# Tail of a decoder step: last expert result copied by two engines, samples combined first and scaled by GpSimd, prompt tiles scaled and stored in halves

## The chip, the cores and the metric

The kernel runs on one core of a Trainium2 chip. The core has TensorE (matrix products, results in PSUM banks ps0 to ps7), VectorE, ScalarE, GpSimd and SyncE, each with its own instruction stream, which meet only at semaphores. SyncE does nothing here but issue transfers. The metric is the device time of one launch in microseconds; lower is better. In the profile PE is TensorE, DVE VectorE, ACT ScalarE, POOL GpSimd and SP SyncE.

## The reference

One decoder layer for 256 prompt tokens and 8 sample tokens (one new token of each of 8 sequences), model width 1024, all in float32: a mixer, a cross-attention, 32 routed experts of which each token takes 4, and a last RMS norm. The end of it is what matters here:

```python
def run_block(args):
    e, idx = args
    xb = x_pad[idx]
    gu = xb @ w_e1[e] + b_e1[e]
    ...
    h = (u + 1.0) * (g * jax.nn.sigmoid(SWIGLU_ALPHA * g))
    return h @ w_e2[e] + b_e2[e]
...
x = x + routed_experts(rms_norm(x, g_moe), moe_w)      # each token: sum over its 4 experts, weighted by gates
...
y_prompt = rms_norm(xp, g_final)                       # x * rsqrt(mean(x*x) + EPS) * g_final
y_sample = rms_norm(xs, g_final)
```

## The kernel before

The work is written out engine by engine. The 32 experts are done in 16 pairs (`PAIRS`), each expert on up to 64 token slots (`CAP`): 8 slots for the samples, 56 for prompt tokens that were gathered by a selection matrix. SyncE streams each expert's weights (first matrix in four transfers, second in two, 2 MB each) through the tile `ring` and two more places. For each expert TensorE multiplies by the first matrix (`up`, L1737), VectorE and ScalarE apply the gated activation, TensorE turns the result (`turn_h`, L1746) and multiplies by the second matrix (`down`, L1756) into bank ps3: 64 slots in partitions 0 to 63 for columns 0 to 511, and in partitions 64 to 127 for columns 512 to 1023. ScalarE's `keep_y` (L779) copies the two halves to `ysb`; the pair's second expert takes rows 64 to 127 of `ysb`.

The running result is the tile `tok`: prompt tiles 0 and 1 (128 tokens each, `tok[:, 0, :]` and `tok[:, 1, :]`) and the samples (`tok[0:8, 2, :]`). A pair's `ysb` is brought back to the prompt tokens by a product with the gates `gT`, two halves of 512 columns for each tile, and VectorE adds them to `tok`. For the last pair these are the lines after `pair(PAIRS - 1)`: TensorE L1820 (four products, one semaphore step of `comb_done` each), VectorE L1268 (four adds). The samples' share of the last pair is two products with `pick_last` (TensorE L1823, added onto what `early_samples` has already put in ps4 and ps5) and two adds (VectorE L1273).

Then comes the last norm, tile by tile. ScalarE squares with a sum (L825) and takes the root (L828); it does the tiles in the order 0, 1, samples. VectorE takes the reciprocal (L1303) and multiplies the whole tile by it and by the final gain `gfin`, which lies in SBUF (L1305). SyncE stores each tile behind it (L444, L446) and waits for all. Each engine works in order. GpSimd loads the bias of each expert (L508) and has nothing more to do after that. Where a routing overflows the slots, a loop over more blocks follows (`n > 0`); in the profiled execution it is passed over.

Of the kernel before, what the change touches and what calls it, by code (L numbers as in the profile page):

```python
# [117 lines left out]
def build(nc, a, outs):  # L118
    ctx = ExitStack()
    with ctx:  # L120
# [168 lines left out]
        smp_chain gates8_ready acc_zeroed sel_ready selg_ready gathered xe_ready gt_turned gt_ready g_clamped u_clamped t_done tu_done h_ready  # L289
        h_turned hT_ready y_ready comb_done acc_done b1_filled b1_used gfin_loaded  # L290
        fin_sq fin_sd fin_rec fin_ready y_stored""".split()
# [31 lines left out]
        def _(sp):  # L323
# [118 lines left out]
            for t in range(2):  # L442
                sp.wait_ge(S["fin_ready"], t + 1)
                sp.dma_start(outs["y_prompt"][0, t * P:(t + 1) * P, :], tok[:, t, :]).then_inc(S["y_stored"], 16)  # L444
            sp.wait_ge(S["fin_ready"], 3)
            sp.dma_start(outs["y_sample"].rearrange("b t d -> (b t) d"), tok[0:NB, 2, :]).then_inc(S["y_stored"], 16)  # L446
            sp.wait_ge(S["y_stored"], 48)
# [6 lines left out]
        def _(pool):  # L454
# [65 lines left out]
            with pool.If(n > 0):  # L520
                pool.wait_ge(S["table_ready"], 1)
                with pool.Fori(0, n) as j:
                    e = pool.value_load(tabi[0:1, 0, bass.ds(j, 1)], min_val=0, max_val=NE - 1)
                    pool.wait_ge(S["b1_used"], j + NE)
                    bias(e)


        @block.scalar
        def _(act):
# [245 lines left out]
            def keep_y(b, e2):  # L775

                act.wait_ge(S["freed"], RING * b + (freed_after(MOE0 - 1) + RING))
                for i in range(2):
# [12 lines left out]
            def pair(q, last=False):  # L791
# [9 lines left out]
                keep_y(2 * q + 1, 1)  # L801
# [18 lines left out]
            for t, (t0, rows) in enumerate(TT):  # L820
# [6 lines left out]
                act.wait_ge(S["fin_sq"], t + 1)  # L827
# [4 lines left out]
        def _(dve):  # L832
# [430 lines left out]
            pair(PAIRS - 1, True)  # L1263
            for t in range(2):
# [5 lines left out]
            dve.wait_ge(S["smp_chain"], 3 + PAIRS)  # L1270
            for i in range(2):
                dst = tok[0:NB, 2, 512 * i:512 * i + 512]
                last = dve.tensor_tensor(dst, dst, ps[LAST_BANKS[2] + i][0:NB, :], ALU.add)  # L1273
            last.then_inc(S["smp_chain"], 1)
# [25 lines left out]
            for t, (t0, rows) in enumerate(TT):  # L1300
                r = slice(0, rows)
                dve.wait_ge(S["fin_sd"], t + 1)
                dve.reciprocal(frs[:, t:t + 1], frs[:, t:t + 1]).then_inc(S["fin_rec"], 1)  # L1303
                dve.wait_ge(S["fin_rec"], t + 2)
                dve.scalar_tensor_tensor(out=tok[r, t, :], in0=tok[r, t, :], scalar=frs[r, t:t + 1], in1=gfin[r, :],  # L1305
                                         op0=ALU.mult, op1=ALU.mult).then_inc(S["fin_ready"], 1)
# [3 lines left out]
        def _(pe):  # L1310
# [506 lines left out]
            pe.wait_ge(S["y_ready"], NE)  # L1817
# [57 lines left out]
```

## Time and profile before

| | us |
|---|---|
| median of 3 runs | 1221.78 (1220.18 to 1224.59) |
| the profiled execution, its own time | 1222.58 |
| its span, first to last instruction | 1221.0 |
| TensorE busy | 1144.9 (94%) |
| VectorE busy | 337.5 (28%) |
| ScalarE busy | 186.2 (15%) |
| GpSimd busy | 45.5 (4%) |
| transfers | 457.43 MB, mean 375 GB/s |

The span counts the instructions of the core; the execution's own time has 1.58 us more around it. Busy shares are means over the whole span; what the end of the kernel waits for is read from the chain of waits and the timeline, whose times count from the start of the span.

### The profile page before, as it was taken

The numbers are of one execution on the slowest core, as the hardware profiler recorded it, in microseconds if no ns is written. First come the engines' busy times: TensorE is split into PE (matmuls) and PEld (weight loads), VectorE is DVE, ScalarE is ACT, GpSimd is POOL, SyncE is SP. The second block draws the span as 40 slices with busy tenths as digits, with TensorE's granted clock in tenths as the row PEclk, the third lists the DMA queues.
The fourth block names the chain that finished last, engine by engine and source line by source line (L and its number), as shares of the span: only waits on it lengthen the run. The fifth ranks groups of instructions, "written<-read, shape, count | busy, mean of one in ns | idle before, by whom it ended". The sixth has DMA issues, their size and how long they took to land.

```text
span 1221.0 us, 14241 instructions
## 1 busy us (share of the span) xinstructions
PE 1144.9 (94%) x5466; PEld 550.5 (45%) x5466; DVE 337.5 (28%) x828; ACT 186.2 (15%) x364; POOL 45.5 (4%) x85
## 2 busy tenths in 40 slices
PE   9999999999999999999989898989898999989896
PEld 7887888684334343333323232323232333333322
DVE  4795529134120212122120202021212121212113
ACT  4205213322011110101101010101010101010102
POOL 4100002000000000000000000000000000000000
PEclk9999999998899999999999999999999999999999
DMA  9398335995999999999999999999999999999993
GB/s 299 109 321 264 142 104 193 390 414 215 420 426 425 429 425 429 428 429 426 428 429 427 427 428 429 427 426 429 428 428 428 427 428 429 429 427 428 426 428 146
DMA packets 65624, 457.43 MB, mean 375 GB/s; under 512 B 5515, under 2 KB 34435, under 8 KB 40885
## 3 DMA queue, kind: packets, MB, share of 16 engines
q1 hardware_dynamic: 62576, 452.00, 90.0%
q10 hardware_dynamic: 1165, 3.04, 0.7%
q0 software_dynamic: 1856, 2.02, 0.6%
q8 instruction: 18, 0.29, 0.1%
q14 instruction: 9, 0.07, 0.0%
HBM read 453.71 MB, written 3.81 MB: 375 GB/s over the span
## 4 chain that ended last, share of the span: by engine, by line
DMA 48%; PE 44%; DVE 5%; ACT 2%; issue 1%; POOL 0%; SPq 0%; ACTq 0%; DVEq 0%; POOLq 0%
DMA ring<-in_w_e 48%; PE ps L1737 17%; PE ps L1400 10%; PE ps L1756 5%; PE ps L1422 3%; DVE ring L1072 2%; PE ps L1713 1%; PE ps L1704 1%; PE ps L1642 1%; PE ps L1340 1%; PE ps L1585 1%; PE ps L1554 1%; PE ps L1314 1%; PE ps L1633 1%; PE ps L1746 1%
## 5 line engine op out<-in xcount | busy, mean ns | idle before, releaser
L1737 PE MATMUL ps<-ring,mixed 128*64 128x512 f32 x1536 | 347.1, 597 | 38.6 <-DMA ring<-in_w_e 38.5
L1756 PE MATMUL ps<-ring,mixed 128*64 128x512 f32 x1024 | 229.7, 602 | 0.7 <-issue 0.7
L1737 PEld LDWEIGHTS ps<-ring,mixed 128*64 128x64 f32 x1536 | 104.6, 137 | 265.3 <-issue 181.0
L1227 DVE TENSOR_SCALAR mixed<-ps 128x512 f32<-128x512 f32 x32 | 22.1, 692 | 590.5 <-PE ps L1737 590.5
L1756 PEld LDWEIGHTS ps<-ring,mixed 128*64 128x64 f32 x1024 | 71.8, 138 | 156.6 <-issue 144.4
L769 ACT ACTIVATE mixed<-mixed 128x512 f32<-128x512 f32 x32 | 20.2, 630 | 516.1 <-DVE mixed L1227 516.1
L1713 PEld LDWEIGHTS ps<-mixed 128*128 128x128 f32 x512 | 63.4, 199 | 24.5 <-issue 24.3
L779 ACT ACTIVATE mixed<-ps 64x512 f32<-64x512 f32 x64 | 37.8, 591 | 229.2 <-PE ps L1756 228.8
L1713 PE MATMUL ps<-mixed 128*128 128x128 f32 x512 | 69.2, 290 | 0.0
L1737 PE MATMUL ps<-mixed 128*64 128x512 f32 x256 | 58.2, 596 | 9.4 <-DMA mixed<-in_w_e 9.4
L1214 DVE SCALAR_TENSOR_TENSOR mixed<-mixed,gates 128x1024 f32<-128x1024 f32 x15 | 19.3, 1285 | 153.2 <-ACT mixed L779 153.2
L1400 PE MATMUL ps<-mixed,ring 128*128 128x264 f32 x256 | 57.6, 387 | 0.4 <-DVE mixed L1106 0.4
L1737 PE MATMUL ps<-low,mixed 128*64 128x512 f32 x256 | 57.9, 593 | 0.0
L1422 PE MATMUL ps<-ring,low 128*128 128x256 f32 x256 | 56.2, 380 | 0.0
L1704 PE MATMUL ps<-mixed 128*128 128x512 f32 x120 | 55.5, 606 | 0.0
L1400 PEld LDWEIGHTS ps<-mixed,ring 128*128 128x128 f32 x256 | 48.6, 190 | 9.1 <-issue 0.6
L1422 PEld LDWEIGHTS ps<-ring,low 128*128 128x128 f32 x256 | 48.7, 190 | 6.5
L508 POOL DMA_DIRECT2D mixed<-in_b_e x32 | 18.2, 567 | 866.9 <-PE ps L1642 849.8
L945 DVE SCALAR_TENSOR_TENSOR mixed<-mixed,par 128x256 f32<-128x256 f32 x120 | 47.6, 468 | 0.0
L1400 PE MATMUL ps<-sq,ring 128*128 128x264 f32 x192 | 44.8, 398 | 0.0
L1400 PEld LDWEIGHTS ps<-sq,ring 128*128 128x128 f32 x192 | 37.6, 196 | 6.7
L1208 DVE TENSOR_TENSOR tok<-tok,ps 128x512 f32<-128x512 f32 x64 | 39.6, 680 | 0.2 <-PE ps L1702 0.2
(320 smaller groups left out, 769.0 us busy)
## 6 DMA issues: line engine op xcount, KB each, us to landing
ring<-in_w_e SPq DMA_DIRECT2D x160, 2048.0 KB, 23.4
low<-in_w_e SPq DMA_DIRECT2D x15, 2048.0 KB, 27.6
mixed<-in_w_e SPq DMA_DIRECT2D x15, 2048.0 KB, 31.9
ring<-in_w_in SPq DMA_DIRECT2D x8, 1024.0 KB, 16.3
ring<-in_cache_mem_k SPq DMA_DIRECT2D x8, 1024.0 KB, 4.8
ring<-in_cache_mem_v SPq DMA_DIRECT2D x7, 1024.0 KB, 7.6
ring<-in_w_k SPq DMA_DIRECT2D x4, 1024.0 KB, 8.7
ring<-in_w_v SPq DMA_DIRECT2D x4, 1024.0 KB, 12.4
```

What stands on the lines that cost most here:

```text
L769: act.activation(tg, g1, ACT.Tanh, scale=ALPHA / 2).then_inc(S["t_done"], 1)
L779: m = act.activation(ysb[CAP * e2:CAP * e2 + CAP, 512 * i:512 * i + 512], ps[3][CAP * i:CAP * i + CAP, :], ACT.Copy)
L945: dve.scalar_tensor_tensor(out=gc[:, c, 0:SEQ], in0=gpad[:, c, bass.ds(w, SEQ)], scalar=par[:, bass.ds(4 * w + (C_WCF + c), 1)], in1=gc[:, ...
L1072: last = dve.tensor_tensor_reduce(key[:, t, h, :], key[:, t, h, :], qb[h][:, HD * b:HD * b + HD], 1.0, 0.0, ALU.mult, ALU.add, sT[:, t, 4 ...
L1208: last = dve.tensor_tensor(dst, dst, ps[bank + i][0:rows, :], ALU.add)
L1227: dve.tensor_scalar(g1, ps[0][:, :], LIMIT, None, ALU.min).then_inc(S["g_clamped"], 1)
L1400: m = pe.matmul(ps[o % 4][:, 0:TOK], wslot(n)[:, k, half * P:(half + 1) * P], (xn if o < 4 else sq)[:, k, :] if kind == "in" else src(k), ...
L1422: m = pe.matmul(ps[KV_BANK[j]][:, 256 * t:256 * t + 256], mn[:, k, P * t:P * t + P], wslot(n)[:, k, :], start=(k == 0), stop=(k == KD - 1))
L1704: m = pe.matmul(ps[bank + i][:, :], gT[:, t0:t0 + P], ysb[:, cols], start=True, stop=True)
L1713: m = pe.matmul(ps[4 + i][:, P * (k % 4):P * (k % 4) + P], xnt[:, t, DEAL[k]], sel[:, t, :], start=(t == 0), stop=(t == 1))
L1737: m = pe.matmul(ps[gu][CAP * i:CAP * i + CAP, :], xeT[:, k, CAP * e2:CAP * e2 + CAP], w[:, D * gu + 512 * i:D * gu + 512 * i + 512], start ...
L1756: m = pe.matmul(ps[3][CAP * i:CAP * i + CAP, :], hTv[:, k % 4, CAP * (k // 4):CAP * (k // 4) + CAP], ring[:, s, D * (k % 2) + 512 * i:D * ...
```

## The change

It has four parts. The last expert's result is copied by ScalarE (columns 0 to 511) and by VectorE (columns 512 to 1023). The samples' products and adds of the last pair are put ahead of those of the prompt tiles, and ScalarE squares the samples first. The samples' last scaling is taken from VectorE and given to GpSimd, as two operations. VectorE scales each prompt tile in two halves of 512 columns, and SyncE stores each half by itself, with the sample store between the two tiles.

```diff
--- before.py
+++ after.py
@@ -286,9 +286,9 @@
         late_loaded qs_turned qs_kept dots_done rs_ready qrow_loaded qb_ready s_chain spv_done osb_kept pick_chain
         o_done part_kept tok_rooted tm_turned tokr_kept xnt_kept logit_done lg_zeroed lg_ready idx_ready eq_ready gate_chain rank_chain block_chain nblk_ready v0_ready ge_ready mask_ready rank_done
         gt0_turned gt0_kept be2_loaded tab_turned tab_ready table_ready
-        smp_chain gates8_ready acc_zeroed sel_ready selg_ready gathered xe_ready gt_turned gt_ready g_clamped u_clamped t_done tu_done h_ready
+        smp_chain gates8_ready acc_zeroed sel_ready selg_ready half_kept gathered xe_ready gt_turned gt_ready g_clamped u_clamped t_done tu_done h_ready
         h_turned hT_ready y_ready comb_done acc_done b1_filled b1_used gfin_loaded
-        fin_sq fin_sd fin_rec fin_ready y_stored""".split()
+        fin_sq fin_sd fin_rec smp_fin fin_ready y_stored""".split()
         S = {n: sem(n) for n in names}
 
         def slot(n):
@@ -439,12 +439,14 @@
                         fill(e, s, used(j + NE - 1, s + 1))
                     rest(e, j + NE)
 
-            for t in range(2):
-                sp.wait_ge(S["fin_ready"], t + 1)
-                sp.dma_start(outs["y_prompt"][0, t * P:(t + 1) * P, :], tok[:, t, :]).then_inc(S["y_stored"], 16)
-            sp.wait_ge(S["fin_ready"], 3)
-            sp.dma_start(outs["y_sample"].rearrange("b t d -> (b t) d"), tok[0:NB, 2, :]).then_inc(S["y_stored"], 16)
-            sp.wait_ge(S["y_stored"], 48)
+            for i in range(4):
+                if i == 2:
+                    sp.wait_ge(S["smp_fin"], 2)
+                    sp.dma_start(outs["y_sample"].rearrange("b t d -> (b t) d"), tok[0:NB, 2, :]).then_inc(S["y_stored"], 16)
+                t, cols = i // 2, slice(512 * (i % 2), 512 * (i % 2) + 512)
+                sp.wait_ge(S["fin_ready"], i + 1)
+                sp.dma_start(outs["y_prompt"][0, t * P:(t + 1) * P, cols], tok[:, t, cols]).then_inc(S["y_stored"], 16)
+            sp.wait_ge(S["y_stored"], 80)
             sp.wait_ge(S["kv_stored"], 32)
             sp.wait_ge(S["rows_stored"], 16 * 6)
             sp.wait_ge(S["caches_shifted"], 32)
@@ -523,6 +525,13 @@
                     e = pool.value_load(tabi[0:1, 0, bass.ds(j, 1)], min_val=0, max_val=NE - 1)
                     pool.wait_ge(S["b1_used"], j + NE)
                     bias(e)
+
+
+            pool.wait_ge(S["gfin_loaded"], 16)
+            pool.wait_ge(S["fin_rec"], 2)
+            pool.tensor_scalar(tok[0:NB, 2, :], tok[0:NB, 2, :], frs[0:NB, 2:3], None, ALU.mult).then_inc(S["smp_fin"], 1)
+            pool.wait_ge(S["smp_fin"], 1)
+            pool.tensor_tensor(tok[0:NB, 2, :], tok[0:NB, 2, :], gfin[0:NB, :], ALU.mult).then_inc(S["smp_fin"], 1)
 
 
         @block.scalar
@@ -772,10 +781,10 @@
                 act.wait_ge(S["h_turned"], b + 1)
                 act.activation(hT, ps[2][:, :], ACT.Copy, scale=0.5).then_inc(S["hT_ready"], 1)
 
-            def keep_y(b, e2):
+            def keep_y(b, e2, shared=False):
 
                 act.wait_ge(S["freed"], RING * b + (freed_after(MOE0 - 1) + RING))
-                for i in range(2):
+                for i in range(1 if shared else 2):
                     m = act.activation(ysb[CAP * e2:CAP * e2 + CAP, 512 * i:512 * i + 512],
                                        ps[3][CAP * i:CAP * i + CAP, :], ACT.Copy)
                 m.then_inc(S["y_ready"], 1)
@@ -798,7 +807,7 @@
                 keep_h(2 * q + 1)
                 if not last:
                     keep_gathered(q + 1)
-                keep_y(2 * q + 1, 1)
+                keep_y(2 * q + 1, 1, last)
 
             with act.Fori(0, PAIRS - 1) as q:
                 pair(q)
@@ -817,14 +826,15 @@
 
             act.wait_ge(S["fin_rec"], 1)
             act.activation(unused, eps[:, 0:1], ACT.Sqrt)
-            for t, (t0, rows) in enumerate(TT):
+            for step, t in enumerate((2, 0, 1)):
+                rows = TT[t][1]
                 if t < 2:
                     act.wait_ge(S["acc_done"], 2 * n + (2 * PAIRS + 1 + t))
                 else:
                     act.wait_ge(S["smp_chain"], 3 + PAIRS + 1)
                 act.activation(xnt[0:rows, t, :], tok[0:rows, t, :], ACT.Square,
                                accum_out=fss[0:rows, t:t + 1]).then_inc(S["fin_sq"], 1)
-                act.wait_ge(S["fin_sq"], t + 1)
+                act.wait_ge(S["fin_sq"], step + 1)
                 act.activation(frs[:, t:t + 1], fss[:, t:t + 1], ACT.Sqrt, bias=eps[:, 0:1], scale=1.0 / D).then_inc(S["fin_sd"], 1)
 
 
@@ -1261,17 +1271,19 @@
             with dve.Fori(1, PAIRS - 1) as q:
                 pair(q)
             pair(PAIRS - 1, True)
+            dve.wait_ge(S["freed"], RING * (NE - 1) + (freed_after(MOE0 - 1) + RING))
+            dve.tensor_copy(ysb[CAP:2 * CAP, 512:D], ps[3][CAP:2 * CAP, :]).then_inc(S["half_kept"], 1)
+            dve.wait_ge(S["smp_chain"], 3 + PAIRS)
+            for i in range(2):
+                dst = tok[0:NB, 2, 512 * i:512 * i + 512]
+                last = dve.tensor_tensor(dst, dst, ps[LAST_BANKS[2] + i][0:NB, :], ALU.add)
+            last.then_inc(S["smp_chain"], 1)
             for t in range(2):
                 for i in range(2):
                     dve.wait_ge(S["comb_done"], 2 * PAIRS + 2 * t + i + 1)
                     dst = tok[:, t, 512 * i:512 * i + 512]
                     last = dve.tensor_tensor(dst, dst, ps[LAST_BANKS[t] + i][:, :], ALU.add)
                 last.then_inc(S["acc_done"], 1)
-            dve.wait_ge(S["smp_chain"], 3 + PAIRS)
-            for i in range(2):
-                dst = tok[0:NB, 2, 512 * i:512 * i + 512]
-                last = dve.tensor_tensor(dst, dst, ps[LAST_BANKS[2] + i][0:NB, :], ALU.add)
-            last.then_inc(S["smp_chain"], 1)
             n = dve.value_load(nblk[0:1, 0:1], min_val=0, max_val=P)
             with dve.If(n > 0):
                 dve.wait_ge(S["tab_ready"], 2)
@@ -1297,13 +1309,16 @@
                         add_round(2 * j + (2 * PAIRS + 4), t, PAIR_BANKS[t])
 
             dve.wait_ge(S["gfin_loaded"], 16)
-            for t, (t0, rows) in enumerate(TT):
-                r = slice(0, rows)
-                dve.wait_ge(S["fin_sd"], t + 1)
+            for step, t in enumerate((2, 0, 1)):
+                dve.wait_ge(S["fin_sd"], step + 1)
                 dve.reciprocal(frs[:, t:t + 1], frs[:, t:t + 1]).then_inc(S["fin_rec"], 1)
-                dve.wait_ge(S["fin_rec"], t + 2)
-                dve.scalar_tensor_tensor(out=tok[r, t, :], in0=tok[r, t, :], scalar=frs[r, t:t + 1], in1=gfin[r, :],
-                                         op0=ALU.mult, op1=ALU.mult).then_inc(S["fin_ready"], 1)
+                if t == 2:
+                    continue
+                dve.wait_ge(S["fin_rec"], step + 2)
+                for i in range(2):
+                    cols = slice(512 * i, 512 * i + 512)
+                    dve.scalar_tensor_tensor(out=tok[:, t, cols], in0=tok[:, t, cols], scalar=frs[:, t:t + 1], in1=gfin[:, cols],
+                                             op0=ALU.mult, op1=ALU.mult).then_inc(S["fin_ready"], 1)
 
 
         @block.tensor
@@ -1815,13 +1830,14 @@
                 pair(q)
             pair(PAIRS - 1, last=True)
             pe.wait_ge(S["y_ready"], NE)
+            pe.wait_ge(S["half_kept"], 1)
+            for i in range(2):
+                m = pe.matmul(ps[LAST_BANKS[2] + i][0:NB, :], pick_last, ysb[:, 512 * i:512 * i + 512], start=False, stop=True)
+            m.then_inc(S["smp_chain"], 1)
             for t in range(2):
                 for i in range(2):
                     pe.matmul(ps[LAST_BANKS[t] + i][:, :], gT[:, P * t:P * t + P], ysb[:, 512 * i:512 * i + 512],
                               start=True, stop=True).then_inc(S["comb_done"], 1)
-            for i in range(2):
-                m = pe.matmul(ps[LAST_BANKS[2] + i][0:NB, :], pick_last, ysb[:, 512 * i:512 * i + 512], start=False, stop=True)
-            m.then_inc(S["smp_chain"], 1)
             pe.wait_ge(S["nblk_ready"], 1)
             n = pe.value_load(nblk[0:1, 0:1], min_val=0, max_val=P)
             with pe.If(n > 0):
```

What follows is the order of instructions before and after on the engines concerned; the brackets name semaphores. First TensorE, from the last down projection to the end of the products, before:

```order
L1756 MATMUL ps<-ring,mixed 64x512 [waits filled8,hT_ready,gt_ready]
L1756 MATMUL ps<-ring,mixed 64x512 x7
L1756 MATMUL ps<-ring,mixed 64x512 [waits filled10]
L1756 MATMUL ps<-ring,mixed 64x512 x7
L1820 MATMUL ps<-mixed 128x512 [waits y_ready]
L1820 MATMUL ps<-mixed 128x512 x3
L1823 MATMUL ps<-mixed,extra 8x512 x2
```

and after the change:

```order
L1771 MATMUL ps<-ring,mixed 64x512 [waits filled8,hT_ready,gt_ready]
L1771 MATMUL ps<-ring,mixed 64x512 x7
L1771 MATMUL ps<-ring,mixed 64x512 [waits filled10]
L1771 MATMUL ps<-ring,mixed 64x512 x7
L1835 MATMUL ps<-mixed,extra 8x512 [waits half_kept,y_ready]
L1835 MATMUL ps<-mixed,extra 8x512
L1839 MATMUL ps<-mixed 128x512 x4
```

The two sample products (8x512) have moved ahead of the four prompt products (128x512), and they now wait for `half_kept`, VectorE's copy, as well as for `y_ready`, ScalarE's.

VectorE from its last activation to the end of the adds, before:

```order
L1230 SCALAR_TENSOR_TENSOR mixed<-mixed 128x512 [waits t_done]
L1233 SCALAR_TENSOR_TENSOR mixed<-mixed 128x512 [waits u_clamped,tu_done]
L1268 TENSOR_TENSOR tok<-tok,ps 128x512 [waits comb_done] x4
L1273 TENSOR_TENSOR tok<-tok,ps 8x512 [waits smp_chain]
L1273 TENSOR_TENSOR tok<-tok,ps 8x512
```

and after:

```order
L1240 SCALAR_TENSOR_TENSOR mixed<-mixed 128x512 [waits t_done]
L1243 SCALAR_TENSOR_TENSOR mixed<-mixed 128x512 [waits u_clamped,tu_done]
L1275 COPY mixed<-ps 64x512 [waits freed]
L1279 TENSOR_TENSOR tok<-tok,ps 8x512 [waits smp_chain]
L1279 TENSOR_TENSOR tok<-tok,ps 8x512
L1285 TENSOR_TENSOR tok<-tok,ps 128x512 [waits comb_done] x4
```

The copy of 64x512 is new, and the sample adds stand ahead of the four prompt adds.

VectorE in the last norm, before:

```order
L1303 RECIPROCAL small<-small 128x1 [waits fin_sd,gfin_loaded]
L1305 SCALAR_TENSOR_TENSOR tok<-tok,small,xn 128x1024 [waits fin_rec]
L1303 RECIPROCAL small<-small 128x1 [waits fin_sd]
L1305 SCALAR_TENSOR_TENSOR tok<-tok,small,xn 128x1024 [waits fin_rec]
L1303 RECIPROCAL small<-small 128x1 [waits fin_sd]
L1305 SCALAR_TENSOR_TENSOR tok<-tok,small,xn 8x1024 [waits fin_rec]
```

and after:

```order
L1314 RECIPROCAL small<-small 128x1 [waits fin_sd,gfin_loaded]
L1314 RECIPROCAL small<-small 128x1 [waits fin_sd]
L1320 SCALAR_TENSOR_TENSOR tok<-tok,small,xn 128x512 [waits fin_rec]
L1320 SCALAR_TENSOR_TENSOR tok<-tok,small,xn 128x512
L1314 RECIPROCAL small<-small 128x1 [waits fin_sd]
L1320 SCALAR_TENSOR_TENSOR tok<-tok,small,xn 128x512 [waits fin_rec]
L1320 SCALAR_TENSOR_TENSOR tok<-tok,small,xn 128x512
```

The two reciprocals that come first are those of the samples and of tile 0; the scaling of 8x1024 is gone, and each of the two wide ones is two of 512 columns. Both operations of the samples are now GpSimd's last (a scaling that waits for `fin_rec`, a product that waits for the scaling by `smp_fin`).

## Rows read from the trace of the kernel before

**Rows 1.** The page, its chain that ended last, shares of the span by engine.

```profile
DMA 48%; PE 44%; DVE 5%; ACT 2%; issue 1%; POOL 0%; SPq 0%; ACTq 0%; DVEq 0%; POOLq 0%
```

**Rows 2.** The chain in order of time, end of the kernel: start us, us, what.

```profile
1165.67 25.61 DMA ring<-in_w_e
...
1199.37 7.10 PE ps L1756 x32
```

**Rows 3.** Timeline of the tail: start us, us, engine line operation, [idle before <-releaser].

```profile
1206.49 1.19 ACT L779 ACTIVATE mixed<-ps 64x512 f32<-64x512 f32 x2 [7.22 <-PE ps L1756]
...
1207.74 3.70 PE L1820 MATMUL ps<-mixed 128*128 128x512 f32 x8 [1.28 <-ACT mixed L779]
...
1208.90 0.69 DVE L1268 TENSOR_TENSOR tok<-tok,ps 128x512 f32<-128x512 f32 x1 [11.07 <-PE ps L1820]
...
1210.48 1.06 ACT L825 ACTIVATE mixed<-tok 128x1024 f32<-128x1024 f32 x1 [1.28 <-DVE tok L1268]
...
1211.37 1.88 PE L1823 MATMUL ps<-mixed,extra 128*8 128x512 f32 x4
...
1211.48 0.69 DVE L1268 TENSOR_TENSOR tok<-tok,ps 128x512 f32<-128x512 f32 x1 [0.17 <-PE ps L1820]
1211.66 0.29 ACT L828 ACTIVATE small<-small,eps 128x1 f32<-128x1 f32 x1
...
1213.29 1.27 DVE L1273 TENSOR_TENSOR tok<-tok,ps 8x512 f32<-8x512 f32 x2 [1.12 <-PE ps L1823]
...
1214.52 0.16 DVE L1303 RECIPROCAL small<-small 128x1 f32<-128x1 f32 x1
...
1214.71 1.29 DVE L1305 SCALAR_TENSOR_TENSOR tok<-tok,small,xn 128x1024 f32<-128x1024 f32 x1
...
1217.50 1.27 DVE L1305 SCALAR_TENSOR_TENSOR tok<-tok,small,xn 8x1024 f32<-8x1024 f32 x1
1218.80 0.34 SPq L446 DMA_DIRECT2D out_y_sample<-tok  x1
```

**Rows 4.** Waits of SyncE from 1150 us: us in total, times, longest us.

```profile
SPq L120 <- DMA out_y_sample<-tok: 1.3, 1, 1.3
```

**Rows 5.** A window of the tail: us; engines busy; PEclk, DMA share, GB/s.

```profile
1217.00:1217.50 0.50, 0.00 (x0) 0.00 (x0) 0.47 (x2) 0.00 (x0) 0.00 (x0) 0.50 0.97 401
```

**Rows 6.** VectorE's groups by shape: count, busy us, mean ns, idle before.

```profile
L1102 DVE COPY mixed<-ps 128x512 f32<-128x512 f32 x2 | 1.3, 686 | 9.8 <-PE ps L1585 9.8
L1022 DVE COPY sq<-ps 11x512 f32<-11x512 f32 x1 | 0.7, 671 | 0.0
L1230 DVE SCALAR_TENSOR_TENSOR mixed<-mixed 128x512 f32<-128x512 f32 x32 | 22.1, 692 | 3.2
```

**Rows 7.** GpSimd's groups by line, at 1024 columns.

```profile
L501 POOL PARTITION_BROADCAST mixed<-mixed x4 | 5.3, 1391 | 152.3 <-DMA mixed<-tok 152.3
L514 POOL MEMSET mixed<- 128x1024 f32 x1 | 0.9, 946 | 41.5 <-ACT mixed L731 41.5
```

**Rows 8.** Timeline in the attention part, VectorE beside GpSimd.

```profile
188.69 2.83 POOL L501 PARTITION_BROADCAST mixed<-mixed  x2 [4.62 <-DMA mixed<-tok]
...
188.98 1.37 DVE L1072 CUSTOM_DVE_ANT_0 ring<-ring,mixed 128x256 f32<-128x256 f32 x1
...
190.28 1.37 DVE L1072 CUSTOM_DVE_ANT_0 ring<-ring,mixed 128x256 f32<-128x256 f32 x1
...
191.58 0.41 DVE L1072 CUSTOM_DVE_ANT_0 ring<-ring,mixed 128x256 f32<-128x256 f32 x1
```

**Rows 9.** Lines L501 and L1072: duration ns min/median/max, first and last start.

```profile
L501 POOL PARTITION_BROADCAST mixed<-mixed x4: 1297/1370/1527, 181.6 to 190.1; - x4
...
L1072 DVE CUSTOM_DVE_ANT_0 ring<-ring,sq x16: 412/414/1371, 198.7 to 206.3; 128x256 f32<-128x256 f32 x16
```

**Rows 10.** Timeline of GpSimd, start-up and its last instruction before the tail.

```profile
27.29 0.18 POOL L474 IOTA iota_s<- 128x56 f32 x1 [7.17 <-issue]
...
1141.41 0.56 POOL L508 DMA_DIRECT2D mixed<-in_b_e  x1 [28.48 <-PE ps L1642]
```

## Prediction

> **What bounds the kernel now.** I read the page first: the chain that ended last runs through transfers for 48% of the span, nearly all of it expert weights, and through TensorE for 44% [rows 1]. The chain of waits in order of time shows where that ends: the last transfer that anything waits for is over at 1191.28 (1165.67 + 25.61), and from then on it is one serial stretch of some 30 us, in which the last down projection ends at 1206.47 [rows 2]. The change touches nothing ahead of that point, so the 1206.5 us before it stay, and the whole question is what the last 14.5 us become.
>
> The timeline of that tail [rows 3] is to be read as four steps. (a) ScalarE copies both halves of the last result in 1.19 us; TensorE starts at 1207.74. (b) Four prompt products, one each 0.86 us (VectorE's four adds start from 1208.90 to 1211.48), then two sample products from 1211.37; VectorE's sample add starts at 1213.29, 1.92 after its products began. (c) VectorE has its first scaled square root at 1211.95 (1211.66 + 0.29) but is held in order by the sample add until 1214.52. (d) Three scalings of about 1.28 us follow back to back, the small sample one last, and end at 1218.77. SyncE issues the sample store at 1218.80, takes 0.34, waits 1.3 for its landing [rows 4], so it is released at 1220.44; another 0.56 closes the span of 1221.0. The two prompt stores move at about 401 GB/s [rows 5] and are hidden until nearly the end.
>
> **Step (a), two engines copy.** ScalarE keeps one 64x512 copy (half of 1.19, so 0.60); VectorE takes the other. The trace has no 64-row copy by VectorE, but a 128x512 one from PSUM takes 0.686 and an 11x512 one 0.671 [rows 6], so rows don't matter and I take 0.67. Both start at 1206.49, TensorE starts at 1206.49 + 0.67 + 0.05 = 1207.21 in place of 1207.74: 0.53 earlier. Bounds: if the two engines hinder each other in the one bank, 0.6 later than that and the gain is nothing.
>
> **Step (b), samples first.** A first add started 1.16 after TensorE (1208.90 - 1207.74) and each further one 0.86 later, so two products are ready 2.02 after the start: sample add at 1209.23, its two parts take 1.27, end 1210.50. Prompt products are ready at 1210.09, 1210.95, 1211.81 and 1212.67; the adds of 0.69 then start at 1210.53, 1211.24, 1211.95 and 1212.69, the last ends at 1213.38. That is 1.21 later than before (1211.48 + 0.69 = 1212.17). ScalarE needs 1.47 a tile (1210.48 to 1211.95): samples from 1210.54 to 1212.01, tile 0 to 1213.50, tile 1 to 1214.99. Nothing on VectorE is held by the sample add any more, yet its first wide scaling now waits for tile 0's root at 1213.50, against 1214.71 at which it started before.
>
> **Step (d) without any interference.** VectorE: sample reciprocal at about 1213.35 for 0.16; tile 0's from 1213.53, scaling at 1213.72. A half takes 0.69 (a 128x512 of this form: 0.692 [rows 6]), so fin halves at 1214.41 and 1215.10; tile 1's reciprocal to 1215.28, its halves at 1216.00 and 1216.69. That is 2.08 ahead of 1218.77, half of it from the sample scaling of 1.27 that left VectorE, the rest from the 1.0 earlier start, less two more fixed costs.
>
> **GpSimd's two operations.** The scaling of 8x1024 and the product with the final gain are new to this engine, and no row has either. Rows are no shorter for few partitions on the other engines (8x1024 takes 1.27 like 128x1024). Nearest rows at 1024 columns [rows 7]: a memset, which reads nothing, 0.95; a broadcast, which reads one input, 1.39. For the one-input scaling I take 1.2, between the two. For the two-input product the floor is 0.95, the ceiling twice the broadcast, 2.75; I take 2.1, since it must read twice. The Trainium skill, GPSIMD Engine Reference, section "Elementwise — side-by-side cycle accounting", states some 2.6 cycles an element for a two-input operation; at the clock on that page this is an estimate of 2.2 us, no run here shows it, and the sum below would end 0.1 later by it.
>
> **Do they hold VectorE up?** Here is the term that decides the sign. In the attention part, VectorE runs a chain of 128x256 operations with two SBUF inputs, each 0.41. While GpSimd runs two broadcasts from 188.69 for 2.83, exactly two of them take 1.37 instead, and the next is back at 0.41 [rows 8]. Nor is that one place: of the sixteen such operations on the next head, beside later broadcasts, the longest took 1.371 at a median of 0.414 [rows 9]. So such an operation isn't slowed in proportion: it waits for nearly the whole GpSimd operation, one per GpSimd operation, and ends 0.13 behind it (the first broadcast took the 1.53 that [rows 9] give as the longest, so 190.22, against 190.35). The wide scaling also reads two SBUF inputs, tile and gain. By these rows its price is: GpSimd's scaling runs 1213.60 to 1214.80; the first half, begun at 1213.72, ends some 0.4 behind it (0.69 less the 0.28 that the blocked 0.41 had already done) at 1215.2. GpSimd's product, ready at 1214.9, gets its turn then, 1215.2 to 1217.3, as the second broadcast did; the second half ends at 1217.7. Reciprocal and two halves free of it: 1217.9, 1218.6, 1219.3. So the 2.08 gained turn into 0.55 lost on VectorE. If the second half gets ahead of the product instead, the product holds tile 1's first half, and the end is the same.
>
> The Trainium skill, SBUF — State Buffer, section "Who interferes with whom", says that a VectorE instruction with two SBUF inputs and a GpSimd instruction that reads SBUF exclude each other for the whole instruction, whoever is first. By that rule, with no overlap at all, both blocked halves would end 0.28 later, so the sum would be 0.56 higher than by the row; the row is what I go by. The adds from PSUM have one SBUF input and are free of it.
>
> **The stores.** In the new order SyncE issues tile 0's halves, then waits for the sample result (1217.3, long before tile 1), then tile 1's halves. So the last issue is at 1219.33. From issue to release the sample store took 1.64; a half tile has 0.23 MB more, 0.57 at 401 GB/s, so 1.64 to 2.2, and I take 1.9. Sum: 1219.33 + 1.9 + 0.56 = 1221.8, against 1221.0: **0.8 us slower** in the profiled execution (own time 1222.58, so 1223.4). That execution stands 0.80 above the median of the runs, 1221.78; on that footing the forecast is 1222.6. Ends: both GpSimd operations at 0.95 and the store at 1.64 give a last half at 1217.9 and a span of 1220.1 (0.9 faster); 1.39 with 2.75 and 2.2 give 1220.1 and 1222.9 (1.9 slower).
>
> **Rivals.**
> 1. No hold-up: the form of scaling here doesn't exclude GpSimd (for it: the rows are of another VectorE operation and another GpSimd operation, and GpSimd works on 8 partitions only). Then VectorE is done at 1216.69, but SyncE waits in order for the sample result at 1213.60 + 1.2 + 0.1 + 2.1 = 1217.0 and issues tile 1's halves at 1217.35 and 1217.7; 1217.7 + 1.9 + 0.56 = 1220.2, 0.8 faster: 1221.0. With GpSimd at 0.95 each it isn't late at all and 1.8 is gained: 1220.0.
> 2. Slower beyond what can be told: GpSimd's first arithmetic after a long pause stalls. The one unexplained GpSimd idle time is 7.17 ahead of an iota, put down to issue [rows 10]. The same here puts the sample result at 1213.6 + 7.2 + 3.3 = 1224.1, and tile 1's stores are queued behind it on SyncE: last issue 1224.8, span 1227.3, 6.3 slower: 1228.1. It crosses 0.3% (3.7 us, about what a measurement of this kernel can tell from no change) only where the stall is over 4.6. Against it: that idle time stood in the start-up, behind a string of transfers issued by the same engine, and here its last issue is at 1141, over 70 us before.
> 3. The shared copy brings nothing (one bank read by two engines): everything 0.5 to 0.6 later than the forecast, 1223.2. Against it: they read different partitions.
>
> **How the numbers follow.** Hold-up as forecast 0.70, no hold-up 0.22, GpSimd stall 0.03, copy brings nothing 0.05. All but the stall lie within 0.3%: the tail has 14.5 us, and no mechanism in it pays or costs 3.7 except that one. So faster 0.03 and slower 0.03 for what the spread between runs (1220.18 to 1224.59) may feign. Range: from rival 1's 1220.0 to the forecast's upper bound, 1222.6 + 1.1 = 1223.7, each widened by some of that spread: 1219.7 to 1224.4. The forecast's own range is 1220.9 to 1223.7.
>
> **What the changed profile would show.** Right: TensorE's sample products at 1207.2 if the down projection ends at 1206.5; four scalings of which two take well over 1 us and two 0.69; GpSimd's two at 1.2 and 2.1; SyncE's last store issue at about 1219.3. Wrong: all four scalings at 0.69 (rival 1), and then the gap before the sample store on SyncE tells whether GpSimd is the new bound; a GpSimd start long after the sample reciprocal (rival 2). The result would be off too if the part before 1206.5 moved by more than the tail can, which would be spread, not this change.

## The result, and the profile after

The changed kernel takes 1226.76 us (median of 20 runs, 1225.60 to 1229.02) against 1222.22 us before (20 runs, 1220.18 to 1225.41): the ratio is 1.0038, 95% interval 1.0032 to 1.0044. That is 4.5 us slower, where 0.8 slower was forecast, and outside the range of 1219.7 to 1224.4.

Since the part before the tail moves by some microseconds from run to run, the tail is compared by itself in all that follows: the time from the end of the last down projection to the end of the span. The chain of waits gives its start (start us, us, what). After the change:

```profile
1164.47 25.62 DMA ring<-in_w_e
...
1198.17 7.10 PE ps L1771 x32
...
1212.91 0.23 DVE small L1314 x2
1213.15 0.14 issue
1213.29 3.37 POOL tok L532
1216.65 0.04 issue
1216.69 2.47 POOLq L120
```

The projection ends at 1205.27, the span at 1223.9: a tail of **18.6 us**, against 14.5 before (1221.0 less 1206.47, [rows 2]). So the tail is 4.1 longer, which is the result but for 0.4, well within the spread of runs. The chain now ends in GpSimd, and its last piece isn't named for an operation but for L120, the end of the program. The timeline of the tail after the change (start us, us, engine line operation, idle before):

```profile
1205.30 0.69 DVE L1275 COPY mixed<-ps 64x512 f32<-64x512 f32 x1 [8.66 <-PE ps L1771]
1206.14 1.88 PE L1835 MATMUL ps<-mixed,extra 128*8 128x512 f32 x4 [0.88 <-DVE mixed L1275]
...
1211.68 0.69 DVE L1285 TENSOR_TENSOR tok<-tok,ps 128x512 f32<-128x512 f32 x1 [0.17 <-PE ps L1839]
...
1212.91 0.22 DVE L1314 RECIPROCAL small<-small 128x1 f32<-128x1 f32 x2 [0.54 <-issue]
1213.17 2.27 DVE L1320 SCALAR_TENSOR_TENSOR tok<-tok,small,xn 128x512 f32<-128x512 f32 x2
1213.29 3.37 POOL L532 TENSOR_SCALAR tok<-tok,small 8x1024 f32<-8x1024 f32 x1 [72.48 <-DVE small L1314]
...
1215.55 1.41 DVE L1320 SCALAR_TENSOR_TENSOR tok<-tok,small,xn 128x512 f32<-128x512 f32 x2
1216.73 2.43 POOL L534 TENSOR_TENSOR tok<-tok,xn 8x1024 f32<-8x1024 f32 x1
1219.19 0.34 SPq L445 DMA_DIRECT2D out_y_sample<-tok  x1
1219.57 0.83 SPq L448 DMA_DIRECT2D out_y_prompt<-tok  x2
```

Beside [rows 3]: TensorE starts 0.87 behind the projection, not 1.27, so the shared copy gains 0.4. VectorE is done at 1216.96, which is 11.7 behind the projection and 0.6 sooner than before. One of its four halves took 1.60, the others some 0.75 (ns min/median/max):

```profile
L1320 DVE SCALAR_TENSOR_TENSOR tok<-tok,small,xn x4: 743/751/1604, 1213.2 to 1216.2; 128x512 f32<-128x512 f32 x4
```

But GpSimd's scaling takes 3.37 us, and its product ends at 1219.16; SyncE has tile 1's two halves ready since 1216.3 and 1216.96 and issues them behind the sample store from 1219.57. And then the line L120, which holds the end of each engine's program (duration ns min/median/max, start):

```profile
L120 DVEq DRAIN  x1: 1449/1449/1449, 1215.6 to 1215.6; - x1
L120 POOLq DRAIN  x1: 6967/6967/6967, 1216.7 to 1216.7; - x1
L120 SPq COMPARE_BRANCH  x1: 41/41/41, 1222.6 to 1222.6; - x1
L120 SPq DRAIN  x1: 13/13/13, 1222.7 to 1222.7; - x1
...
L120 POOLq EVENT_SEMAPHORE  x2: 17/17/17, 1223.7 to 1223.8; - x2
```

SyncE sees its last store landed at 1222.6. GpSimd's drain starts with its product and runs 6.97 us, to 1223.66, 4.5 behind the product's end; only then do the engines meet and the span closes. The trace of before has a drain too, at a place where it cost nothing. It stood behind a transfer issue there, and ended 7.2 behind it (1141.41 + 0.56, [rows 10]):

```profile
L120 POOLq DRAIN  x1: 6642/6642/6642, 1142.5 to 1142.5; - x1
L120 SPq COMPARE_BRANCH  x1: 41/41/41, 1220.6 to 1220.6; - x1
```

So three things stand in the tail after: operations of GpSimd that are longer than forecast, stores that queue behind them on SyncE, and the drain. The first two make one path, which ends in SyncE's release; the drain makes another. In the trace of before the span ends 0.4 behind the release (1220.6, 1221.0). Counted so, SyncE's path would end the changed kernel at 1223.0, a tail of 17.7; the drain ends it at 1223.9, a tail of 18.6. So the trace puts 3.2 us of the loss on the late stores and only the last 0.9 on the drain, if the drain counts at all. The experiments test that.

### The profile page after: what moved, and what is told of

It reads as the page before. It is cut to its first block, busy times and chain, and to the rows that moved or that the text cites. A ratio compares the mean times of both kernels' runs of the same rounds, so it can differ in the third digit from the quotient of the medians.

```text
span 1223.9 us, 14250 instructions
## 1 busy us (share of the span) xinstructions
PE 1142.3 (93%) x5466; PEld 548.7 (45%) x5466; DVE 338.0 (28%) x830; ACT 185.2 (15%) x363; POOL 51.5 (4%) x87
## 4 chain that ended last, share of the span: by engine, by line
DMA 48%; PE 44%; DVE 5%; ACT 1%; issue 1%; POOL 0%; POOLq 0%; SPq 0%; ACTq 0%; DVEq 0%
DMA ring<-in_w_e 48%; PE ps L1752 17%; PE ps L1415 10%; PE ps L1771 5%; PE ps L1437 3%; DVE ring L1082 2%; PE ps L1728 1%; PE ps L1719 1%; PE ps L1657 1%; PE ps L1355 1%; PE ps L1600 1%; PE ps L1329 1%; PE ps L1569 1%; PE ps L1761 0%; PE ps L1648 0%
## 5 line engine op out<-in xcount | busy, mean ns | idle before, releaser
L1752 PEld LDWEIGHTS ps<-mixed 128*64 128x64 f32 x256 | 17.5, 137 | 49.2 <-issue 30.8
```

The lines of the kernel that those rows point to most:

```text
L1752: m = pe.matmul(ps[gu][CAP * i:CAP * i + CAP, :], xeT[:, k, CAP * e2:CAP * e2 + CAP], w[:, D * gu + 512 * i:D * gu + 512 * i + 512], start ...
```

## The experiments

Each kernel is the changed one or the one before with one edit. Tails are from one profiled execution of each. Kernels whose tails end with the same work came out within 0.1 of each other: 14.5 in two, 18.5 to 18.6 in three.

**The sample store last.** Edit on SyncE:

```diff
-                if i == 2:
-                    sp.wait_ge(S["smp_fin"], 2)
-                    sp.dma_start(outs["y_sample"]..., tok[0:NB, 2, :])
...
+            sp.wait_ge(S["smp_fin"], 2)
+            sp.dma_start(outs["y_sample"]..., tok[0:NB, 2, :])
```

> The changed kernel with one thing moved: SyncE stores the samples last instead of between the two prompt tiles. Tail is the time from the end of the last down projection to the end of the span: 14.5 us before the change, 18.6 after. Drain theory (GpSimd's own drain at the end of its program ends some 4.5 us behind its last operation and closes the span): tile 1's two stores are issued about 3 us earlier, SyncE is done about 1.5 us earlier, and the span does not move: tail 18.6, within 0.2. Queue theory (the stores of tile 1 held behind the sample store set the end): tail 17.0, time 1.5 us less than the changed kernel's.

1226.4 us (5 runs), ratio to the kernel before 1.0037 (1.0024 to 1.0049), the same as the change. The tail was 19.1. SyncE was released at 1220.3, and the drain ran on:

```profile
L120 POOLq DRAIN  x1: 6872/6872/6872, 1216.1 to 1216.1; - x1
L120 SPq COMPARE_BRANCH  x1: 41/41/41, 1220.3 to 1220.3; - x1
```

The queue theory falls: SyncE was done 2.7 us ahead of the drain's end (1223.0), and that gained nothing, so the drain closes the span. It doesn't follow that the queue is harmless: in the changed kernel its path ends only 0.9 ahead of the drain's. The tail is even 0.5 longer, because GpSimd's scaling took 3.95 here:

```profile
1212.02 1.42 DVE L1319 SCALAR_TENSOR_TENSOR tok<-tok,small,xn 128x512 f32<-128x512 f32 x2
1212.13 3.95 POOL L531 TENSOR_SCALAR tok<-tok,small 8x1024 f32<-8x1024 f32 x1 [72.52 <-DVE small L1313]
...
1213.54 1.99 DVE L1319 SCALAR_TENSOR_TENSOR tok<-tok,small,xn 128x512 f32<-128x512 f32 x2
```

Both engines lose here: VectorE 0.6 in its second pair of halves, GpSimd 0.6. Why it was the second pair here and the first in the changed kernel, the traces don't show.

**The samples scaled by VectorE, last.**

```diff
-            pool.tensor_scalar(tok[0:NB, 2, :], tok[0:NB, 2, :], frs[0:NB, 2:3], None, ALU.mult)
...
-            pool.tensor_tensor(tok[0:NB, 2, :], tok[0:NB, 2, :], gfin[0:NB, :], ALU.mult)
...
+                if t == 2:
+                    dve.scalar_tensor_tensor(out=tok[0:NB, 2, :], in0=tok[0:NB, 2, :], scalar=frs[0:NB, 2:3],
+                                             in1=gfin[0:NB, :], op0=ALU.mult, op1=ALU.mult)
```

> The changed kernel without GpSimd: VectorE does the samples' last scaling, in one operation, last, and SyncE stores them last; the copy by two engines, the samples' products first and the halves stay. If all of the loss is GpSimd's (drain and long operations together): tail about 14.4 us and a time within 0.1% of the kernel before. If the loss lies in the new order (samples first delays the prompt tiles) or in the halved scalings and stores: tail 15.5 or more. VectorE's halves at 0.69 us each if the 0.75 and 1.60 of the changed kernel came from GpSimd beside it; still 0.75 if a half of a row costs that.

1222.12 us (12 runs), ratio 0.9993 (0.9984 to 1.0002): no change that can be told. The tail was 14.4 (projection ended at 1207.98, span 1222.35). All of the loss is GpSimd's; the rest of the change, with the samples scaled and stored last, is worth 0.1 us together. And the halves take the same without GpSimd:

```profile
1215.82 1.41 DVE L1316 SCALAR_TENSOR_TENSOR tok<-tok,small,xn 128x512 f32<-128x512 f32 x2
...
1217.34 1.42 DVE L1316 SCALAR_TENSOR_TENSOR tok<-tok,small,xn 128x512 f32<-128x512 f32 x2
```

So 1.41 a pair is what halves cost here, and only the 2.27 of tile 0 in the changed kernel was a hold-up, of 0.86.

**A memset behind the last scaling**, in the kernel before:

```diff
+            pool.wait_ge(S["fin_ready"], 3)
+            pool.memset(extra[0:NB, 84:96], 0.0)
```

> The kernel before, with one GpSimd memset of 8x12 elements on scratch columns that waits for VectorE's last scaling; nothing waits for it but the end of the program. Drain theory: the drain behind it ends some 4.5 us after it, at about 4.7 us past the last scaling where the span of before ended 2.2 past it: 2.5 us slower, 0.2%. Rival (the long drain in the changed kernel belongs to GpSimd arithmetic or to its reads, not to a plain write): no change.

1225.49 us (11 runs), ratio 1.0022 (1.0012 to 1.0032); the tail was 17.2, 2.7 more than before. An operation of 0.1 us that nothing reads makes this kernel 0.2% slower:

```profile
1217.95 0.34 SPq L446 DMA_DIRECT2D out_y_sample<-tok  x1
1217.99 0.10 POOL L528 MEMSET extra<- 8x12 f32 x1 [76.84 <-DVE tok L1308]
```

```profile
L120 POOLq DRAIN  x1: 4602/4602/4602, 1218.0 to 1218.0; - x1
L120 SPq COMPARE_BRANCH  x1: 41/41/41, 1219.8 to 1219.8; - x1
```

Again the drain ends 4.5 behind the last operation (4.60 less 0.12), as behind the product, and SyncE had been released 2.8 before that. **The control**, the same memset some 10 us earlier:

```diff
-            pool.wait_ge(S["fin_ready"], 3)
+            pool.wait_ge(S["comb_done"], 2 * PAIRS + 1)
```

> Control for the memset behind the last scaling: the same GpSimd memset in the kernel before, but waiting for the first prompt product of the last pair, some 2.5 us behind the last down projection. Drain theory: it drains until about 7.2, far from the end, tail 14.5, time as before (within 0.1%). If an added GpSimd instruction at the end of the program costs by itself, wherever it runs: 2.5 us slower, as there.

1222.17 us (10 runs), ratio 1.0002 (0.9990 to 1.0014), tail 14.5. The memset stood at 1208.56, its drain (4602 ns again) was over at 1213.1. It is the place of GpSimd's last instruction that costs, not its presence.

**GpSimd warmed up** with a small scaling and a small product 70 us ahead, on 8x12 elements of scratch (`wu`):

```diff
+            pool.memset(wu, 1.0)
+            pool.tensor_scalar(wu, wu, ones[0:NB, 0:1], None, ALU.mult)
+            pool.tensor_tensor(wu, wu, wu, ALU.mult)
```

> The changed kernel, with a scaling and a product of 8x12 elements put on GpSimd some 70 us ahead, on scratch columns. First-use theory (2 of the 3.37 us of GpSimd's scaling are paid once): the scaling of 8x1024 takes 1.2 to 1.5, the sample result is 2 us earlier, the drain too, tail 16.6. Inherent theory (the operation costs 3.3 ns an element on this engine): it takes 3.37 again, tail 18.6.

1227.59 us (6 runs), ratio 1.0037 (1.0026 to 1.0049), tail 18.6. The first-use theory falls:

```profile
1145.75 0.10 POOL L531 MEMSET extra<- 8x12 f32 x1 [0.57 <-issue]
1153.03 0.68 POOL L533 TENSOR_SCALAR extra<-extra,ones 8x12 f32<-8x12 f32 x1 [7.18 <-issue]
1153.79 0.20 POOL L535 TENSOR_TENSOR extra<-extra 8x12 f32<-8x12 f32 x1
1217.62 3.38 POOL L538 TENSOR_SCALAR tok<-tok,small 8x1024 f32<-8x1024 f32 x1 [63.63 <-DVE small L1320]
1221.09 2.44 POOL L540 TENSOR_TENSOR tok<-tok,xn 8x1024 f32<-8x1024 f32 x1
```

From 12 to 1024 columns the scaling grows by 2.70 us, 2.7 ns a column, and the product by 2.24, 2.2 ns a column. The scaling's price is in its columns. There is a first-use cost of another kind, 7.18 us in which GpSimd stood still ahead of the small scaling. Each kernel has two configuring instructions on the scaling's line, here and in the changed kernel:

```profile
L533 POOLq MODIFY_POOL_CONFIG  x2: 1/1/1, 1145.9 to 1145.9; - x2
```

```profile
L532 POOLq MODIFY_POOL_CONFIG  x2: 5/5/5, 1141.4 to 1141.5; - x2
```

Here the 7.18 us follow them; in the changed kernel they stand at 1141.4, at the head of the 72 us in which GpSimd waited anyway, and its scaling started 0.16 behind the reciprocal. So it is most likely that the stall fell into that wait; the trace doesn't show it by itself.

**The scaling written as a product** (the first line added), **and by a constant** (the second, in another kernel).

```diff
-            pool.tensor_scalar(..., frs[0:NB, 2:3], None, ALU.mult)
+            pool.tensor_tensor(..., frs[0:NB, 2:3].to_broadcast([NB, D]), ALU.mult)
+            pool.tensor_scalar(..., 0.5, None, ALU.mult)
```

> The changed kernel with GpSimd's scaling by a number per partition written as a product with that number spread over the row (one element per partition read again and again). If the operation with a number per partition is what is slow on this engine (3.37 us): 2.4 us, like the product with the gain, tail 17.7. If the first of two late operations costs more, whichever it is: 3.3 again, tail 18.6.

> The changed kernel with GpSimd scaling the samples by the constant 0.5 in place of the reciprocal root, so y_sample is not normalised and the number per partition is not read. If a one-input operation runs near one element a cycle once no number is fetched: 1 to 1.4 us, tail 16.6. If the slowness is in the operation's loop: 3.3, tail 18.6.

Both only profiled. The kernel with the constant leaves the norm of the samples out. By the constant: 3.29, tail 18.5. As a product: tail 17.9, and the timeline:

```profile
1213.32 3.05 DVE L1320 SCALAR_TENSOR_TENSOR tok<-tok,small,xn 128x512 f32<-128x512 f32 x2
1213.38 2.43 POOL L532 TENSOR_TENSOR tok<-tok,small 8x1024 f32<-8x1024 f32 x1 [72.45 <-DVE small L1314]
...
1214.09 2.63 SPq L448 DMA_DIRECT2D out_y_prompt<-tok  x2
1215.89 2.67 POOL L534 TENSOR_TENSOR tok<-tok,xn 8x1024 f32<-8x1024 f32 x1
...
1216.47 3.30 DVE L1320 SCALAR_TENSOR_TENSOR tok<-tok,small,xn 128x512 f32<-128x512 f32 x2
```

GpSimd's operation with one input and a number is what is slow, wherever the number comes from; the product over 1024 columns needs 2.43. And here is the hold-up of the kind that was forecast: each product kept one of VectorE's halves waiting, the pairs took 3.05 and 3.30 in place of 1.41, so 1.64 and 1.89 more. The first pair ended at 1216.37, 0.56 behind the product's end at 1215.81. A half takes 0.75, so all but some 0.2 of the held half was done after GpSimd was through. It was the second half: the first was over when SyncE issued its store at 1214.09, though the product had begun at 1213.38, beside it. The scaling holds VectorE for only 0.6 to 0.9 of its 3.3 to 3.9 us.

The tail fell by 0.7 only, with the scaling 0.9 shorter: the second product took 2.67 and ended at 1218.56, and the drain again closed the span 4.7 behind it.

**The copy by two engines alone**, on the kernel before, only profiled:

> The kernel before with only the first part of the change, the last result copied by ScalarE and VectorE. The changed kernel's trace has TensorE start 0.86 us behind the last down projection where before it was 1.27, so tail 14.1 us, 0.4 less. If the copies were not on the path: 14.5.

Its edit is the diff's lines on `keep_y`, `half_kept` and the copy of 64x512. Tail 14.1 (projection ended at 1208.24, span 1222.35), TensorE started 0.87 behind the projection. This part gives its 0.4.

**Whole tiles, no GpSimd**, only profiled: the kernel in which VectorE scales the samples, with one operation and one store for each tile.

```diff
-                for i in range(2):
-                    cols = slice(512 * i, 512 * i + 512)
-                    dve.scalar_tensor_tensor(out=tok[:, t, cols], ...)
+                dve.scalar_tensor_tensor(out=tok[r, t, :], ...)
```

> The changed kernel without GpSimd and without the halves: VectorE scales tile 0, tile 1 and the samples whole, three stores, samples last. The kernel without GpSimd but with halves had a tail of 14.4 us. A half costs VectorE 0.08 us more than half a tile, twice: if the halves give nothing at the end (the sample store is last), tail 14.2 to 14.3. If the earlier first half matters for the queue of transfers: 14.6 or more.

Tail 14.1 (1208.18 to 1222.29), 0.3 less than with halves, where 0.1 to 0.2 was expected: with the sample store last the halves give nothing and cost 0.3. It is the same 14.1 as with the shared copy alone, so the samples' place ahead of the prompt tiles shows no gain either.

**GpSimd's product early, ScalarE scales.** The gain can be multiplied in before the root is known:

```diff
+            pool.wait_ge(S["smp_chain"], 3 + PAIRS + 1)
+            pool.tensor_tensor(acc[0:NB, :], tok[0:NB, 2, :], gfin[0:NB, :], ALU.mult).then_inc(S["smp_fin"], 1)
...
+            act.wait_ge(S["fin_rec"], 2)
+            act.wait_ge(S["smp_fin"], 1)
+            act.activation(acc[0:NB, :], acc[0:NB, :], ACT.Copy, scale=frs[0:NB, 2:3]).then_inc(S["smp_fin"], 1)
```

> GpSimd's work put where its drain is covered: right behind the samples' last add it multiplies the samples by the final gain into scratch (one product, 2.4 us), while ScalarE squares; ScalarE, free after the last root, scales that by the reciprocal; VectorE scales the prompt tiles in halves; SyncE stores the samples between the tiles. Drain theory: GpSimd's product starts 4.1 us behind the last down projection and ends at 6.5, its drain at 11.0, ahead of the stores; the last half is issued at 10.9, so tail 13.1 to 13.3 us, 1.3 less than before: time about 0.1% below the kernel before. If a late GpSimd product costs in another way too (it holds VectorE's adds, or its drain is longer here): tail over 14.5.

> The kernel with GpSimd's product by the gain early, ScalarE's scaling of the samples and no work of GpSimd at the end, now with the prompt tiles scaled and stored whole. With halves its tail was 13.95 us, not 13.1: SyncE was released 2.85 us behind the issue of the last half (256 KB), where the kernel before needed 2.5 from the issue of a whole tile to its last byte. If stores in halves land more slowly: last whole store issued at 10.7 us, tail 13.5, about 0.1% below the kernel before. If the landing of two stores in a row is what costs, whatever their size: 13.9 to 14.2.

With halves: 1221.53 us (11 runs), ratio 0.9995 (0.9986 to 1.0005), tail 13.9. With whole tiles: 1222.0 (11 runs), ratio 0.9992 (0.9983 to 1.0002), tail 14.3. Both misses: neither can be told from the kernel before, and the tails expected were 13.1 to 13.3, and 13.5 for whole tiles. The drain did what the theory says:

```profile
1212.07 2.36 POOL L532 TENSOR_TENSOR mixed<-tok,xn 8x1024 f32<-8x1024 f32 x1 [68.66 <-DVE tok L1280]
...
1213.40 0.69 DVE L1286 TENSOR_TENSOR tok<-tok,ps 128x512 f32<-128x512 f32 x1 [0.17 <-PE ps L1840]
...
1218.05 0.99 SPq L448 DMA_DIRECT2D out_y_prompt<-tok  x2
```

```profile
L120 POOLq DRAIN  x1: 6892/6892/6892, 1212.0 to 1212.0; - x1
L120 SPq COMPARE_BRANCH  x1: 41/41/41, 1221.4 to 1221.4; - x1
```

It was over at 1218.9, ahead of the landing, and VectorE's adds from PSUM kept their 0.69 beside the product. What took the gain is the landing: the second half was issued at 1218.71 (the pair's 0.99 ends at 1219.04, an issue is 0.33), and SyncE was released 2.7 behind that. With whole tiles the last issue was at 1214.57 and the release at 1217.9, 3.3 later; the small store that comes last in the kernel before needs 1.8. So the last issue came 1.5 and 1.7 sooner behind the projection than before, and less than half of that was paid.

What the end follows is rather the first store. It was issued at (kernel before, halves, whole tiles):

```profile
1216.03 1.73 SPq L444 DMA_DIRECT2D out_y_prompt<-tok  x2
```

```profile
1216.53 1.00 SPq L448 DMA_DIRECT2D out_y_prompt<-tok  x2
```

```profile
1213.18 0.36 SPq L447 DMA_DIRECT2D out_y_prompt<-tok  x1
```

From there to the release it is 4.6, 4.9 and 4.7 us, and in between the transfers hardly pause; with halves (us; engines busy; PEclk, DMA share, GB/s):

```profile
1217.50:1221.00 3.50, 0.00 (x0) 0.00 (x0) 1.18 (x2) 0.00 (x0) 0.00 (x0) 0.64 0.86 297
```

The first issue stood 9.6 behind the projection before, and 8.7 and 9.2 in these two. So a last store that is issued sooner only waits longer behind the ones ahead. This is read from the traces; no run tests it alone.

## Why the prediction was wrong

Two steps failed. The larger is in "GpSimd's two operations": "For the one-input scaling I take 1.2", where the scaling measured 3.37. The other is the last term of the sum, in "The stores": "Sum: 1219.33 + 1.9 + 0.56", and in the reading of the kernel before "another 0.56 closes the span". It took for granted that the end is set by SyncE's last landing, whichever engine works last, and put GpSimd's drain at nothing. The drain was in the trace of before, 6.64 us at 1142.5, and was not looked at, because only work in the tail was. The drain gives the end as product's end + 4.5 + 0.2.

How much each is worth follows from the two paths. The forecast was a tail of 15.3. With everything as forecast (product's end at 1217.3, 10.8 behind the projection), the drain alone would have given 15.5. With GpSimd's work as measured and no drain, SyncE's path would have given 17.7. Both together give the 18.6. So of the 3.3 us that the forecast lacks, 2.4 stand in SyncE's path, and 0.9 in the drain. Of the 2.4, 1.8 are the last issue behind GpSimd's late result (14.7 behind the projection, forecast 12.9), the rest a slower landing. The terms:

- **GpSimd's operations.** Taken at 1.2 and 2.1, measured 3.37 and 2.43. The product was in its bounds; the scaling was not: its bounds were two other operations (a write, a broadcast), and the real one costs 2.7 ns a column. This is 2.2 of the 3.1 us by which the sample result was later than forecast (1219.16, 13.9 behind the projection, against 10.8). Another 0.9 is a late start, most of it VectorE's 0.54 idle between the last add and the first reciprocal, where it reads `nblk`; the sum had passed over that. The page of the Trainium skill that was weighed, GPSIMD Engine Reference, section "Elementwise — side-by-side cycle accounting", gives 2.6 cycles an element for two inputs; the product's 2.2 ns a column agrees (at the 1.2 GHz of that page, 2.7 cycles).
- **Hold-up of VectorE.** Forecast as 2.6 in all, measured 0.86: one half, by the scaling, for a quarter of its length; the product began when VectorE was nearly through. So VectorE ended 11.7 behind the projection, not 12.9 as forecast. The mechanism is real and was about rightly sized for a product (1.64 and 1.89 where it was tried, the held half ending 0.56 behind the product where 0.4 was forecast), but it was not what made the kernel slow. The rule of the Trainium skill, SBUF — State Buffer, section "Who interferes with whom", says that such a VectorE and such a GpSimd instruction exclude each other for the whole instruction, whoever is first; the trace agrees for the product and the half behind it, to within 0.2 of its end. It doesn't agree for the scaling, and not for the half that was running when the first product began: neither was longer for it (0.75 and 2.43).
- **Step (a)** was right: 0.53 forecast, 0.40 measured, confirmed alone. **Step (b)** was right within 0.2: last add ends 7.1 behind the projection, forecast 6.9. **Step (d)**: a half of the wide scaling takes 0.75, not 0.69; the row used for it was of another form.
- **The stores.** From last issue to release 1.9 was taken with bounds 1.64 to 2.2; measured 2.6 here (last issue 1219.98, released 1222.6), and 2.7 and 3.3 in the last pair of experiments. By the same mark, the branch at L120, the sample store of the kernel before needed 1.8, and the close behind it 0.4 in place of 0.56.
- **Rival 1** had the path right: SyncE waited in order for the sample result and issued tile 1's halves behind it. It took that result at 10.5 behind the projection, where it came at 13.9, and so called it a gain.
- **Rival 2**, a GpSimd stall, was named as the only thing that could cost 3.7 us, with the right queue behind it. There was a stall of just that length (7.18 in the warmed kernel), but most likely ahead of the wait, where it is free. The same queue passed on a delay of another origin; the drain was on no list.

What is shown: without GpSimd the tail is 14.4; a late memset alone costs 2.7; an early one nothing; the order of the stores nothing while the drain ends last. The split of the loss into 3.2 and 0.9 is worked out from one trace; no run has the changed kernel without its drain. What stays open: why GpSimd's scaling is slower than its product, and what it does in the three quarters of its time in which it doesn't hold VectorE; that would need the inside of its program.

## What to carry to other kernels

GpSimd's last instruction had a price behind it that the busy times don't show, 4.5 us, where VectorE's drain ended 0.1 behind its last half (1215.6 + 1.45, 1216.96): look at the line of the program's end for each engine's drain, and count from the last instruction of each, not only from the last store. Work moved to an engine that had long been done is not free, since it moves that engine's end into the tail; if GpSimd must help, its part should have ended at least 4.5 us before SyncE's last release, as in the two kernels with the gain early. And an operation that the trace of before doesn't show should be bounded by what it costs per column, not by other operations that happen to have the same width.

## What the runs showed of the hardware

- GpSimd's drain at the end of the program ended 4.5 us behind its last operation in every kernel in which one stood there: 6.97 less 2.47 behind a product, 4.60 less 0.12 behind a memset of 0.10 us. Behind a transfer issue, as in the kernel before, it was 7.2.
- GpSimd's scaling of 8x1024 float32: 3.37 (3.38 warmed, 3.29 by a constant, 3.95 in the kernel that stores the samples last); its product 2.33 to 2.44, 2.67 beside VectorE's blocked half.
- Between a memset and the first scaling GpSimd stood still for 7.18 us, in the one kernel that shows it.
- ScalarE and VectorE read two partition halves of one PSUM bank at once at 0.59 and 0.69 us: ScalarE's two copies alone took 1.19, a 128x512 copy of VectorE's 0.69 ([rows 6]).
